# A hand-ordered attention trunk on one core: other places for single instructions, output stores by halves

## The chip, the cores and the metric

The kernel runs on one core of one Trainium2 chip. The metric is the device time of one execution in microseconds (us): 1213.29 us before the change, the median of three runs (1212.85 to 1214.43). TensorE (PE in the profile) multiplies matrices, with its weight loads shown apart (PEld). VectorE is DVE, ScalarE is ACT, GpSimd is POOL, and SyncE (SP) issues most DMAs. Each engine works through its own list of instructions in order; semaphores join the lists.

## The reference, cut to what matters

Two layers over 16 meta tokens and 1024 tokens, width 1024. Each layer adds to h the product of w_out with two gated attention groups; at the end comes one more norm.

```
def hybrid_layer(h, pos, norm_g, w_in, w_out, sinks):
    u = rmsnorm(h, norm_g)
    proj = jnp.einsum('bld,de->ble', u, w_in)
    sb_q, sb_k, sb_v, sb_g, sw_q, sw_k, sw_v, sw_g = jnp.split(proj, splits, axis=-1)
    sb_o = stick_breaking_attention(sb_q, sb_k, sb_v) * silu(sb_g)      # 8 heads, strictly causal
    qr, kr = rope(sw_q, pos), rope(sw_k, pos)
    sw_o = sliding_window_gqa(qr, kr, sw_v, sinks) * silu(sw_g)         # window 128, sinks
    mix = jnp.concatenate([sb_o, sw_o], axis=-1)
    return h + jnp.einsum('ble,ed->bld', mix, w_out)

def reference(...):
    h = concatenate([meta, x])
    for l in range(2):
        h = hybrid_layer(h, pos, norm_g[l], w_in[l], w_out[l], sinks[l])
    return rmsnorm(h, final_norm_g)[:, 16:]
```

## The kernel before, in words

Tokens lie along the free dimension, in three chunks of 400, 384 and 256 (c = 0, 1, 2); features lie on partitions. Weights come in tiles of 128 output features: 26 for w_in, then 8 for w_out. Every projection of a tile on a chunk is done to nearly full float32 precision by three passes over 8 row blocks k: high weights times high input, high weights times low input, low weights times high input, so 24 matmuls. The input's halves are UH and UL, the weights' are WH and WL. A tile's weights are split on VectorE by split_w (line 1424): a CAST to WH (line 1430), then WL as the rest (line 1434). This pair is called the weight pair below. The norm scales a chunk in four parts of two row blocks: "scale" on VectorE (line 1382), "high" on ScalarE (the copy to UH, line 1092), "low" on VectorE (UL, line 1392). The first projection of a layer asks for the four UL parts one after another, each before two of its row blocks.

One list of steps per layer (layer_steps, line 137) sets the order of everything. Each engine walks the same list and issues its own share of each step, so moving a step in the list moves its instructions on every engine that has a part in it. The list follows these stages:

1. First projections (v, g of pair 0), with the norm of the chunks between them. In layer 0 the input is also transposed (in_turn), copied (in_copy: half on ScalarE, half on VectorE), squared for the norm (in_square, ScalarE) and the norm's numbers spread over partitions (in_row, on TensorE). start_steps orders layer 0's start.
2. Stick-breaking attention over 4 pairs of heads, with the next projections merged in.
3. Sliding stage (swa_attention, line 209): 18 units, 9 for each head pair. A unit n has the scores SZ on TensorE; on VectorE the peak (3 or 5 small instructions, lines 1562 to 1570); on ScalarE the exponentials (line 1269); on VectorE the weighing SD (4 instructions, lines 1578 to 1587); on TensorE the turn ST and the values SAV; on VectorE the taking of the result. Between them stand projections (one for each unit, two for the first), rotations (rope_add, rope_high, rope_low) and the weight pairs of later tiles. Near its end stand gates and the splitting of the attention's result into UH and UL, which are the input of w_out.
4. Output projections, each with "add" (h is updated, line 1453; the semaphore h_ready counts 24 of them in a layer), squares and their sum. At the layer boundary boundary_steps puts the next layer's norm of chunk 0 between the last projections.
5. Tail (out_steps): final norm, a transposing matmul for each block of 128 tokens (out_turn, line 1043), scaled copies of the two halves of its 1024 columns (ScalarE the first 512, VectorE the last 512), and one store of 512 KB a block.

WITHIN names small matmuls that stand inside a projection, by row block. proj_slot (line 825) makes the second layer's first two projections wait for the last add of the layer before.

## Time and profile before

| | |
|---|---|
| median of three runs | 1213.29 us (1212.85 to 1214.43) |
| the profiled execution's own time | 1215.04 us |
| its span, first to last instruction | 1213.2 us |
| PE busy | 1174.4 us, 97% |
| DVE busy | 688.3 us, 57% |
| ACT busy | 435.8 us, 36% |

The span leaves out 1.8 us that lie around the instructions. With TensorE busy 97% of the span, its idle time is small: about 39 us in some forty places, and the places matter more than the sums. A row of the timeline shows the idle time just before an instruction in brackets, with the instruction or DMA that ended it.

### The profile page before, as it was taken

The numbers are of one execution on the slowest core, as the hardware profiler recorded it, in microseconds if no ns is written. First come the engines' busy times: TensorE is split into PE (matmuls) and PEld (weight loads), VectorE is DVE, ScalarE is ACT, GpSimd is POOL, SyncE is SP. The second block draws the span as 40 slices with busy tenths as digits, with TensorE's granted clock in tenths as the row PEclk, the third lists the DMA queues.
The fourth block names the chain that finished last, engine by engine and source line by source line (L and its number), as shares of the span: only waits on it lengthen the run. The fifth ranks groups of instructions, "written<-read, shape, count | busy, mean of one in ns | idle before, by whom it ended". The sixth has DMA issues, their size and how long they took to land.

```text
span 1213.2 us, 22513 instructions
## 1 busy us (share of the span) xinstructions
PE 1174.4 (97%) x8922; PEld 1074.2 (89%) x8922; DVE 688.3 (57%) x1370; ACT 435.8 (36%) x1189; POOL 2.6 (0%) x5
## 2 busy tenths in 40 slices
PE   6999999999999999999989999999999999999998
PEld 6988888988888888899989888888888888888998
DVE  6646464455457567754574564655544855766533
ACT  7323333333344344521231333333334433554113
POOL 0000000000000000000000000000000000000000
PEclk9999999999999999999999999999999999999999
DMA  6611010101021021141321110101011212104203
GB/s 213 219 36 36 19 36 18 36 19 36 21 56 44 23 57 50 41 172 35 141 70 54 34 36 19 36 19 36 18 36 25 64 36 45 49 14 171 70 5 140
DMA packets 101687, 69.31 MB, mean 57 GB/s; under 512 B 37824, under 2 KB 95168, under 8 KB 101584
## 3 DMA queue, kind: packets, MB, share of 16 engines
q1 hardware_dynamic: 100720, 66.55, 18.2%
q8 instruction: 72, 1.18, 0.4%
q10 hardware_dynamic: 864, 1.32, 0.4%
q14 instruction: 31, 0.25, 0.1%
HBM read 49.82 MB, written 12.71 MB: 52 GB/s over the span
## 4 chain that ended last, share of the span: by engine, by line
PE 89%; DVE 5%; issue 2%; ACT 2%; DMA 1%; SPq 0%; ACTq 0%; DVEq 0%
PE psum L867 41%; PE psum L855 20%; PE psum L917 7%; PE psum L946 6%; PE psum L929 6%; PE psum L978 2%; PE psum L1043 1%; PE psum L990 1%; PE psum L1015 1%; PE psum L1008 1%; DVE mix L1382 1%; DMA vT<-in_x 1%; PE psum L959 1%; PE psum L888 1%; DVE UL L1392 1%
## 5 line engine op out<-in xcount | busy, mean ns | idle before, releaser
L867 PE MATMUL psum<-UH,WH 128*128 128x384 f32 (+2 forms) x1632 | 538.5, 330 | 10.1 <-DVE UL L1392 4.9
L867 PE MATMUL psum<-UL,WH 128*128 128x384 f32 (+2 forms) x1632 | 524.6, 321 | 0.0
L855 PE MATMUL psum<-UH,WL 128*128 128x384 f32 (+2 forms) x1632 | 517.9, 320 | 0.0
L867 PEld LDWEIGHTS psum<-UH,WH 128*128 128x128 f32 x1632 | 308.4, 189 | 19.9 <-issue 9.0
L867 PEld LDWEIGHTS psum<-UL,WH 128*128 128x128 f32 x1632 | 309.1, 189 | 0.1
L855 PEld LDWEIGHTS psum<-UH,WL 128*128 128x128 f32 x1632 | 308.3, 189 | 0.0
L1255 ACT ACTIVATE PT<-psum 128x512 f32<-128x512 f32 (+5 forms) x260 | 116.7, 492 | 20.0 <-PE psum L929 18.3
L1246 ACT ACTIVATE X<-psum 128x264 f32<-128x264 f32 (+9 forms) x240 | 91.1, 431 | 78.2 <-PE psum L917 77.8
L1514 DVE TENSOR_TENSOR_SCAN X<-X,stick 16x16 f32<-16x16 f32 (+5 forms) x144 | 100.4, 736 | 24.7 <-ACT X L1246 24.3
L929 PE MATMUL psum<-ident,X 128*128 128x128 f32 x576 | 91.1, 283 | 3.7 <-ACT Vn L1209 2.7
L1517 DVE TENSOR_TENSOR_SCAN X<-X 128x352 f32<-128x352 f32 (+4 forms) x96 | 86.3, 939 | 7.7 <-ACT X L1246 7.7
L929 PEld LDWEIGHTS psum<-ident,X 128*128 128x128 f32 x576 | 61.9, 141 | 27.4 <-issue 23.1
L946 PE MATMUL psum<-PT,Vn 128*64 128x128 f32 (+1 forms) x1152 | 83.8, 281 | 0.0
L1434 DVE TENSOR_TENSOR WL<-w_raw,WH 128x1024 fp32r<-128x1024 f32 x67 | 82.1, 1226 | 2.3
L946 PEld LDWEIGHTS psum<-PT,Vn 128*64 128x64 f32 (+1 forms) x1152 | 61.1, 136 | 18.4 <-issue 18.2
L1137 ACT ACTIVATE mix<-X 128x400 f32<-128x400 f32 (+2 forms) x48 | 23.3, 493 | 130.0 <-DVE X L1453 127.8
L1453 DVE TENSOR_TENSOR X<-psum,X 128x400 f32<-128x400 f32 (+2 forms) x48 | 24.8, 517 | 77.0 <-PE psum L855 76.8
L1544 DVE SCALAR_TENSOR_TENSOR mix<-psum,v_end,mix 128x128 f32<-128x128 f32 (+1 forms) x72 | 23.9, 332 | 78.1 <-PE psum L959 78.0
L1430 DVE CAST WH<-w_raw 128x1024 fp32r<-128x1024 f32 x68 | 46.6, 685 | 24.3 <-issue 14.5
L917 PE MATMUL psum<-qk_even 64*128 64x264 f32 (+9 forms) x360 | 46.3, 342 | 3.7 <-DVE qk_even L1467 2.0
L917 PE MATMUL psum<-qk_odd 64*128 64x264 f32 (+9 forms) x360 | 46.4, 342 | 2.2 <-ACT X L1246 1.7
L1467 DVE TENSOR_TENSOR qk_even<-psum,qk_even 128x400 fp32r<-128x400 f32 (+2 forms) x24 | 12.4, 519 | 60.5 <-ACT qk_even L1164 32.0
(171 smaller groups left out, 1000.7 us busy)
## 6 DMA issues: line engine op xcount, KB each, us to landing
w_raw<-in_w_in SPq DMA_DIRECT2D x36, 512.0 KB, 3.8
h_spill<-X SPq DMA_DIRECT2D x16, 520.0 KB, 6.5
X<-h_spill SPq DMA_DIRECT2D x16, 520.0 KB, 5.2
w_raw<-in_w_in SPq DMA_DIRECT2D x32, 256.0 KB, 3.7
w_raw<-in_w_out SPq DMA_DIRECT2D x16, 256.0 KB, 2.9
w_raw<-in_w_out SPq DMA_DIRECT2D x32, 128.0 KB, 3.2
vT<-dvT SPq DMA_DIRECT2D x40, 50.0 KB, 2.0
vT<-dvT SPq DMA_DIRECT2D x40, 48.0 KB, 2.0
```

What stands on the lines that cost most here:

```text
L855: return pe.matmul(out_columns, WL[:, j % 2, k, :], UH[:, k, uses], start=False, stop=(k == KT - 1))
L867: pe.matmul(out_columns, WH[:, j % 2, k, :], u[:, k, uses], start=(k == 0 and u is UH), stop=False)
L917: ins = pe.matmul(z_bank[0:n_queries(b), h, 0:hi - lo], QK[rows, q, queries], QK[rows, k, lo:hi], start=(i == 0), stop=(i == 2))
L929: ins = pe.transpose(bank[:, i * nq:(i + 1) * nq], weights(p, b, h)[:, a:a + 128], ident[:])
L946: ins = pe.matmul(o[64 * h:64 * h + 64, 0:nq], Vn[keys, 9 * (p % 2) + t, 64 * h:64 * h + 64], PT[keys, slots[h] % PT_RING, i * nq:(i + 1) ...
L1246: act.activation(weights(p, b, h)[0:n_queries(b), lo:hi], z_bank[0:n_queries(b), h, 0:hi - lo], ACT.Sigmoid, scale=-SCALE).then_inc(z_read ...
L1255: act.activation(PT[0:rows, slot % PT_RING, 0:width], t_bank[use % T_RING][0:rows, 0:width], ACT.Copy)\
L1430: dve.tensor_copy(WH[:, j % 2, :, :], w_raw[:, j % 2, :, :]).then_inc(wh_made.sem, 1)
L1434: dve.tensor_tensor(WL[:, j % 2, :, :], w_raw[:, j % 2, :, :], WH[:, j % 2, :, :].bitcast(F32), ALU.subtract).then_inc(wl_made.sem, 1)
L1453: dve.tensor_tensor(X[:, t, chunk_uses(c)], proj_bank[use % 2][:, 0:CHUNKS[c][1]], X[:, t, chunk_uses(c)], ALU.add).then_inc(h_ready.sem, 1)
L1514: ins = dve.tensor_tensor_scan(down, down, edge, 1.0, ALU.mult, ALU.max)
L1517: ins = dve.tensor_tensor_scan(down, down, down, P[0:nq, hi:hi + 1], ALU.mult, ALU.bypass)
```

## The change

Five kinds of edits, with no arithmetic changed.

- Start of layer 0: ScalarE's squares stand behind the "high" copies they stood ahead of; the row of norm numbers of chunk 1 goes into the last pass of the first projection; the second tile's weight pair is pulled apart, with its second half behind two parts of the next norm.
- Layer boundary: the norm numbers of chunk 1 and the CAST of tile 0 move ahead of the last two UL parts, with WL behind them; the second tile's WL moves behind chunk 1's scaling; the first projection of layer 1 waits for the 23rd add and not for the 24th.
- Opening of the sliding stage: the scores of units 0 and 1 each stand ahead of the projection they stood behind.
- Sliding stage: the weight pairs of tiles up to the first of w_out move from behind a unit's values to behind the next unit's weighing. There are five such pairs in each layer.
- Tail: the last sums stand between the halves of block 7's turn; each store is split in two of 256 KB, the first waiting for ScalarE's half alone.

```diff
@@ start_steps
-    spread = {c0[0]: [S[4]], c0[2]: [S[5]], c0[4]: [C[4]], c0[5]: [S[6]], c0[7]: [C[5]], c0[8]: [S[7]], c0[10]: [S[8]]}
+    spread = {c0[2]: [S[4]], c0[4]: [C[4]], c0[5]: [S[5]], c0[7]: [C[5]], c0[8]: [S[6]], c0[10]: [S[7], S[8]]}
...
-    steps += [C[6], ("in_root", 1), ("in_refine", 1)] + v[0] + [T[8], ("in_row", 1), ("in_row", 2), ("split_w", 1)]
-    spread = {c1[1]: [C[7]], c1[6]: g[0], c1[8]: [C[8]]}
+    steps += [C[6], ("in_root", 1), ("in_refine", 1), ("split_w", 1, "high")] + v[0] + [T[8], ("in_row", 2)]
+    spread = {c1[1]: [("split_w", 1, "low"), C[7]], c1[6]: g[0], c1[8]: [C[8]]}
@@ layer_steps
-            start = [("split_w", 1)] + v[0] + c1[:4] + [("norm", 2, 0)] + c1[4:7] + g[0] + c1[7:]
+            start = [("split_w", 1, "high")] + v[0] + c1[:3] + [("split_w", 1, "low")] + c1[3:4] + [("norm", 2, 0)]
+            start += c1[4:7] + g[0] + c1[7:]
@@ swa_attention
-        out = fill[0] + [("SZ", 0), ("SD", 0)] + fill[1] + [("SZ", 1)]
-        fill = fill[2:]
+        out = [("SZ", 0), ("SD", 0)] + fill[0] + [("SZ", 1)] + fill[1]
+        fill, weights_next = fill[2:], []
...
-            out += extra.get(n, []) + ropes + [step for step in task if step not in late + ropes]
+            out += extra.get(n, []) + ropes + weights_next + [step for step in task if step not in late + ropes]
...
-            out += [("SAV", n)] + late
+            weights_next = [step for step in late if step[0] == "split_w" and step[1] <= IN_TILES]
+            out += [("SAV", n)] + [step for step in late if step not in weights_next]
...
-    tail[0] = flush + tail[0]
-    steps += swa_attention(tail + [[("proj", IN_TILES + i, c)] for i, c in EARLY_OUTS])
+    steps += flush + swa_attention(tail + [[("proj", IN_TILES + i, c)] for i, c in EARLY_OUTS])
@@ boundary_steps
-            (KT - 1, 1): c0[5:],
-            (KT - 2, 2): [("norm", 1, 1), ("split_w", TILES)]}.get((i, c), [])
+            (KT - 1, 1): c0[5:8] + [("norm", 1, 1), c0[8]],
+            (KT - 2, 2): [("split_w", TILES, "high")] + c0[9:] + [("split_w", TILES, "low")]}.get((i, c), [])
@@ out_steps
-            (KT - 1, 2): [("out_turn", 7), ("out_sum", 2), ("out_root", 2), ("out_copy", 7)] + blocks(8, 9)}.get((i, c), [])
+            (KT - 1, 2): [("out_turn", 7), ("out_root", 2), ("out_copy", 7)] + blocks(8, 9)}.get((i, c), [])
@@ WITHIN
-          ("proj", 0, 0): {4: [("norm_row", 1, 0), ("in_turn", 6)], 6: [("in_turn", 7)]},
+          ("proj", 0, 0): {4: [("norm_row", 1, 0), ("in_turn", 6)], 6: [("in_turn", 7)], KT + 5: [("in_row", 1)]},
@@ sync, the stores
                 sp.wait_ge(out_ready_a, b)
+                sp.dma_start(out[128 * (b - 1):128 * b, 0:512], staged_out(b)[:, 0:512]).then_inc(out_stored, 16)
                 sp.wait_ge(out_ready_v, b)
-                sp.dma_start(out[128 * (b - 1):128 * b, :], staged_out(b)).then_inc(out_stored, 16)
-            sp.wait_ge(out_stored, 16 * (BLOCKS - 1))
+                sp.dma_start(out[128 * (b - 1):128 * b, 512:1024], staged_out(b)[:, 512:1024]).then_inc(out_stored, 16)
+            sp.wait_ge(out_stored, 32 * (BLOCKS - 1))
@@ proj_slot
-                        pe.wait_ge(h_ready.sem, h_ready.at(l, 0))
+                        pe.wait_ge(h_ready.sem, h_ready.at(l, use - 1))
@@ project, in the last pass
+                            if l == 0 and KT + k in WITHIN.get(step, {}):
+                                in_rows(1)
@@ out_turn
+                        if b == 7 and half == 0:
+                            out_sums(2)
@@ split_w: part "high" is the CAST with its waits, part "low" the rest
-                def split_w(j):
+                def split_w(j, part=None):
```

The order of VectorE at the layer boundary, before. X<-psum is an add, small<-psum and small<-small refine the norm numbers of chunk 1, dvT<-dvT,mix sums squares.

```order
L1382 SCALAR_TENSOR_TENSOR mix<-X,par,psum 128x400
L1392 TENSOR_TENSOR UL<-mix,UH 128x2x400 [waits u_scaled,uh_made] x2
L1453 TENSOR_TENSOR X<-psum,X 128x256 [waits h_back0,proj_full]
L1363 SCALAR_TENSOR_TENSOR small<-psum,small 128x3 [waits rooted]
L1366 SCALAR_TENSOR_TENSOR small<-small 128x3 [waits refined]
L1369 SCALAR_TENSOR_TENSOR small<-small 128x3 [waits refined]
L1430 CAST WH<-w_raw 128x1024 [waits wl_made,proj_full,w_landed0]
L1434 TENSOR_TENSOR WL<-w_raw,WH 128x1024 [waits wl_made,wh_made]
L1453 TENSOR_TENSOR X<-psum,X 128x256 [waits h_back1,proj_full]
```

And the same place in the changed kernel.

```order
L1388 SCALAR_TENSOR_TENSOR mix<-X,par,psum 128x400
L1369 SCALAR_TENSOR_TENSOR small<-psum,small 128x3 [waits rooted]
L1372 SCALAR_TENSOR_TENSOR small<-small 128x3 [waits refined]
L1375 SCALAR_TENSOR_TENSOR small<-small 128x3 [waits refined]
L1460 TENSOR_TENSOR X<-psum,X 128x256 [waits h_back0,proj_full]
L1437 CAST WH<-w_raw 128x1024 [waits wl_made,proj_full,w_landed0]
L1398 TENSOR_TENSOR UL<-mix,UH 128x2x400 [waits u_scaled,uh_made] x2
L1441 TENSOR_TENSOR WL<-w_raw,WH 128x1024 [waits wl_made,wh_made]
L1460 TENSOR_TENSOR X<-psum,X 128x256 [waits h_back1,proj_full]
```

The numbers, the 23rd add and the CAST now stand ahead of the last two UL parts; the 24th add still comes last.

VectorE near the end of the sliding stage of layer 0, before: the taking of unit 13's values, the weight pair of w_out's first tile, the weighing of unit 15, the last UL part of chunk 0, the gate and the peak of unit 16.

```order
L1604 COPY mix<-psum 128x2x128 [waits av_done]
L1430 CAST WH<-w_raw 128x1024 [waits wl_made,proj_full,w_landed0]
L1434 TENSOR_TENSOR WL<-w_raw,WH 128x1024 [waits wl_made,wh_made]
L1578 TENSOR_TENSOR small<-small 128x4 [waits z_read,sink_exp]
L1579 RECIPROCAL small<-small 128x4 [waits dve_order]
L1583 TENSOR_TENSOR P_late<-P_late,small 128x4x16 [waits dve_order]
L1587 TENSOR_TENSOR P_late<-P_late,small 128x4x128 [waits dve_order]
L1618 TENSOR_TENSOR UL<-mix,UH 128x2x400 [waits mh_made]
L1479 SCALAR_TENSOR_TENSOR X<-X,psum 128x256 [waits g_act]
```

And the same place in the changed kernel.

```order
L1611 COPY mix<-psum 128x2x128 [waits av_done]
L1585 TENSOR_TENSOR small<-small 128x4 [waits z_read,sink_exp]
L1586 RECIPROCAL small<-small 128x4 [waits dve_order]
L1590 TENSOR_TENSOR P_late<-P_late,small 128x4x16 [waits dve_order]
L1594 TENSOR_TENSOR P_late<-P_late,small 128x4x128 [waits dve_order]
L1625 TENSOR_TENSOR UL<-mix,UH 128x2x400 [waits mh_made]
L1437 CAST WH<-w_raw 128x1024 [waits wl_made,proj_full,w_landed0]
L1441 TENSOR_TENSOR WL<-w_raw,WH 128x1024 [waits wl_made,wh_made]
L1486 SCALAR_TENSOR_TENSOR X<-X,psum 128x256 [waits g_act]
```

The weight pair has moved behind the weighing and the UL part, and stands between them and the gate.

## Rows read from the trace of the kernel before

**Rows 1.** The page: busy us of each engine (share of the span) xinstructions.

```profile
PE 1174.4 (97%) x8922; PEld 1074.2 (89%) x8922; DVE 688.3 (57%) x1370; ACT 435.8 (36%) x1189; POOL 2.6 (0%) x5
```

**Rows 2.** TensorE's waits, whole span: who, for whom, us in total, times, longest.

```profile
PE psum L867 <- issue: 3.2, 1, 3.2
...
PE psum L990 <- DVE P_early L1587: 2.2, 2, 1.1
...
PE psum L867 <- DVE X L1453: 2.0, 2, 1.0
PE psum L978 <- DVE SQ L1552: 1.9, 2, 1.0
PE psum L978 <- ACT P_late L1269: 1.3, 2, 0.7
...
PE psum L978 <- ACT P_early L1269: 0.7, 2, 0.5
```

**Rows 3.** Windows: PE, PEld, DVE, ACT, POOL busy us (instructions), granted clock, DMA, GB/s.

```profile
613.30:616.70 3.40, 3.40 (x13) 3.27 (x12) 2.86 (x5) 0.00 (x0) 0.00 (x0) 0.50 1.02 308
463.10:466.50 3.40, 3.40 (x19) 3.35 (x17) 2.81 (x9) 2.38 (x11) 0.00 (x0) 0.50 0.11 29
```

**Rows 4.** Timeline, layer boundary: start, us, instruction, xcount, [idle before, releaser].

```profile
606.78 2.02 DVE L1392 TENSOR_TENSOR UL<-mix,UH 128x800 fp32r<-128x800 f32 x2
609.77 0.16 DVE L1363 SCALAR_TENSOR_TENSOR small<-psum,small 128x3 f32<-128x3 f32 x1 [0.64 <-ACT small L1084]
612.14 0.42 DVE L1453 TENSOR_TENSOR X<-psum,X 128x256 f32<-128x256 f32 x1
612.66 0.42 PE L867 MATMUL psum<-UH,WH 128*128 128x400 f32 x1 [3.18 <-issue]
615.83 2.19 DVE L1382 SCALAR_TENSOR_TENSOR mix<-X,par,psum 128x384 f32<-128x384 f32 x4 [0.50 <-PE psum L794]
623.96 0.34 PE L867 MATMUL psum<-UH,WH 128*128 128x384 f32 x1
```

**Rows 5.** The weight pair's two instructions, whole span: ns min/median/max, first and last start.

```profile
L1430 DVE CAST WH<-w_raw x68: 655/684/695, 11.7 to 1170.4; 128x1024 fp32r<-128x1024 f32 x68
L1434 DVE TENSOR_TENSOR WL<-w_raw,WH x67: 1224/1226/1227, 24.3 to 1171.1; 128x1024 fp32r<-128x1024 f32 x67
```

**Rows 6.** Timeline, opening of the sliding stage, layer 0.

```profile
395.30 0.64 DVE L1552 TENSOR_TENSOR SQ<-dvT,SQ 128x16 fp32r<-128x16 f32 x2
395.69 0.45 PE L867 MATMUL psum<-UH,WH 128*128 128x400 f32 x1
407.36 0.66 PE L990 MATMUL psum<-ident,P_early 128*128 128x128 f32 x4 [1.11 <-DVE P_early L1587]
```

**Rows 7.** Timeline, end of the sliding stage, layer 0.

```profile
503.85 0.68 DVE L1430 CAST WH<-w_raw 128x1024 fp32r<-128x1024 f32 x1
505.22 0.85 ACT L1255 ACTIVATE PT<-psum 128x512 f32<-128x512 f32 x2
505.71 0.15 DVE L1578 TENSOR_TENSOR small<-small 128x4 f32<-128x4 f32 x1
506.98 0.98 DVE L1618 TENSOR_TENSOR UL<-mix,UH 128x800 fp32r<-128x800 f32 x1
508.11 0.42 PE L867 MATMUL psum<-UH,WH 128*128 128x400 f32 x1
522.77 0.44 PE L867 MATMUL psum<-UH,WH 128*128 128x384 f32 x1 [0.97 <-DVE X L1453]
```

**Rows 8.** Timeline, start of layer 0.

```profile
15.06 0.99 DVE L1392 TENSOR_TENSOR UL<-mix,UH 128x800 fp32r<-128x800 f32 x1 [0.55 <-ACT UH L1092]
18.69 0.45 PE L867 MATMUL psum<-UH,WH 128*128 128x400 f32 x1 [1.52 <-DVE UL L1392]
```

**Rows 9.** DMA issues: out<-in, queue, xcount, KB each, median us to landing.

```profile
out<-w_raw SPq DMA_DIRECT2D x1, 512.0 KB, 3.0
vT<-dvT SPq DMA_DIRECT2D x40, 50.0 KB, 2.0
```

More of the change, by code:

```diff
@@ L757, in _ @@
                 for step in LAYER_STEPS[l]:
-                    if step[0] == "split_w" and step[1] + 2 < TILES:
+                    if step[0] == "split_w" and step[1] + 2 < TILES and step[2:] != ("high",):
                         load(step[1] + 2)
@@ L1422, in _ @@
                 link = chain.link
-                def split_w(j):
-                    dve.wait_ge(w_landed[j % 2].sem, w_landed[j % 2].at(l + j // TILES, landed(j % TILES)))
-                    if j >= 2:
-                        dve.wait_ge(proj_full.sem, proj_full.at(l, PROJ_AT["proj", j - 2, 2] + 1))
-                    if l or j >= 2:
-                        dve.wait_ge(wl_made.sem, wl_made.at(l, j - 1))
-                    dve.tensor_copy(WH[:, j % 2, :, :], w_raw[:, j % 2, :, :]).then_inc(wh_made.sem, 1)
-                    if l or j:
+                def split_w(j, part=None):
+                    if part != "low":
+                        dve.wait_ge(w_landed[j % 2].sem, w_landed[j % 2].at(l + j // TILES, landed(j % TILES)))
+                        if j >= 2:
+                            dve.wait_ge(proj_full.sem, proj_full.at(l, PROJ_AT["proj", j - 2, 2] + 1))
+                        if l or j >= 2:
+                            dve.wait_ge(wl_made.sem, wl_made.at(l, j - 1))
+                        dve.tensor_copy(WH[:, j % 2, :, :], w_raw[:, j % 2, :, :]).then_inc(wh_made.sem, 1)
+                    if (l or j) and part != "high":
                         dve.wait_ge(wh_made.sem, wh_made.at(l, j + 1))
@@ L1657, in _ @@
                     elif kind == "split_w":
-                        split_w(step[1])
+                        split_w(*step[1:])
                     elif kind == "norm":
```

## The prediction, written before the changed kernel had run

> **What bounds the kernel now.** Read the page first: TensorE is busy 97% of the span, 1174.4 us of 1213.2 [rows 1]. Nothing in the change takes a matmul away, so all it can give is part of TensorE's idle time, some 39 us, and whatever time a low clock adds. So the second view is the list of TensorE's waits [rows 2]. The edits touch these: 3.2 us at the layer boundary; 2.2 and 0.7 at the opening of the sliding stage; 1.9 in its middle; 1.3 and 2.0 at its end. Except for the first, each is two waits, one in each layer. The third view is the windows [rows 3]: twice, for 3.4 us each, the granted clock is 0.50, that is 1.2 GHz for 2.4. Such a stretch does half its work, so it costs 1.7 us. One stands right behind the 3.2 us wait at the boundary, the other behind the wait in the middle of layer 0's sliding stage. Last comes the timeline of VectorE at each place, since VectorE ends most of these waits: there the question is whether VectorE itself waits (then its order can be mended) or is busy all through (then moving work only moves the bill).
>
> **Layer boundary: -3.6 us.** TensorE ended layer 0's last projection at 612.66 - 3.18 = 609.5 and began layer 1's first at 612.66, right behind the add that VectorE began at 612.14 [rows 4]. The profile names no releaser, but the code has the wait: the 24th h_ready. That add came late because two UL parts (2.0 us from 606.8), the chunk's numbers (which waited 0.64 for ScalarE), a weight pair and another add stood ahead of it. Now TensorE wants only the 23rd add and the CAST. VectorE from 606.8: three small instructions to 607.4, the 23rd add (0.42) to 607.8, CAST (0.69) to 608.5 [rows 4, 5]. Both are there at 609.5, so this wait ends at nothing. The two UL parts end at 609.5 and 610.4; they are wanted by the fifth and seventh of eight row blocks, 1.5 us and 2.5 us into the projection: in time. WL ends at 611.6, wanted after 16 matmuls at about 612.7: in time. The 24th add ends near 612.0, wanted at 614: in time.
>
> What is late next: on VectorE follow the sums (0.8, to 612.8), CAST (613.4), four scalings (2.19, to 615.6), the WL that was moved behind them (616.8), a UL part (0.96, to 617.8) and chunk 2's numbers (0.6, to 618.4). The second projection wants those numbers before its last row block. Before, the two projections took 623.96 - 612.66 = 11.3 us, 1.7 of it the low clock's: 9.6 at full clock. From 609.5 TensorE would be through at 619.1, and at that row block about 2.1 us sooner, at 617.0. So it waits 1.4 us and is through at 620.4, against 623.96: 3.6 us gained, the 1.7 of the clock included. Bounds: 4.9 (3.2 + 1.7, the new wait hidden) and 1.9 (the new wait brings a low stretch of its own).
>
> **Opening of the sliding stage: -2.4 us.** With unit 0's scores ahead of a projection, the chain scores, peak, exponentials, weighing (11.7 us from 395.69 to the turn at 407.36, with two projections in it) runs beside one projection more. Its two waits in each layer, 2.9 us in both [rows 2], go. The price: the scores need the low half of a rotated query, which VectorE ends at 395.30 + 0.64 = 395.94, and TensorE is there at 395.69 [rows 6]; 0.25 a layer. The tanh and the gates of the moved projections stand behind the exponentials, but the projection that wants their bank begins five microseconds later. Value 2.4; bounds 0 (the chain is only moved) and 2.9.
>
> **Middle: -1.9 us, and the clock's 1.7 in this execution.** The wait is for a rotation's low half (L1552). A weight pair, 0.68 + 1.23 = 1.91 us [rows 5], stood ahead of it on VectorE and now stands behind it. The wait was 0.96, so it goes whole in both layers: 1.9 [rows 2]. The pair ends 1.9 us later, ahead of a wait for scores that VectorE had there anyway. In layer 0 the low stretch from 463.1 goes with the wait [rows 3]; I count it apart, since layer 1's equal wait had none. Bounds 0 and 1.9.
>
> The Trainium skill (TensorE: Matmul & The Clock Gate, "What's actually happening") says that the gate's window runs free of the program. By that, equal waits may or may not meet a low stretch, and this trace's two agree. It changes no term; it speaks for the spread of a run's time.
>
> **End of the sliding stage: +3.2 us.** Here the same move costs. Before, VectorE did the pair of w_out's first tile from 503.85, while ScalarE was still at the exponentials (it went on to the next work at 505.22); the weighing began at 505.71, just behind the pair [rows 7]. Now VectorE idles until the exponentials are done, about 505.4, weighs (1.35) and does the UL part (0.98, to 507.7), and only then the pair: CAST to 508.4, WL to 509.6. TensorE wants that very tile at 508.11, so it waits 0.3 for WH and 0.8 for WL. And VectorE has from there no slack: gate, peak, second pair, weighing, two UL parts, peak follow each other without a break, and end in the add for which TensorE waits 0.97 at 522.77 [rows 7]. All of it comes 1.91 - 0.3 = 1.6 us later, and TensorE's 1.1 us of waits lie inside that. So 1.6 a layer, 3.2. Bounds: 0 and 3.8 (both pairs whole). The other four moved pairs of a layer stand where projections leave VectorE room: 0, or with that room gone 1.6 each.
>
> **Start of layer 0: -0.5 us.** VectorE waited 0.55 for ScalarE's UH, which stood behind a square [rows 8]; that square is now behind. VectorE then ends each UL part about 0.55 sooner, and TensorE's wait of 1.52 for one shrinks as much. The row of numbers in the last pass finds them only just ready (0.3 lost, made good by VectorE's earlier scaling). Bounds 0 and 0.8.
>
> **Tail: -0.7 us.** The earlier sums free block 7's copies, but the last copy waits for the same last matmul. What is left is the last store: 256 KB for 512, with the first half already gone. 512 KB landed in 3.0 us and 50 KB in 2.0 [rows 9]; on the line between, 256 KB take 2.4. Without the store of block 7 beside it, some 0.1 less. Bounds 0 and 1.0.
>
> The Trainium skill (DMA: Bandwidth & Descriptors, "Bandwidth") tells you to batch DMAs into larger ones. By that rule halving would be a loss; with these rows only the last landing counts, and 2.0 of its 3.0 us are there at 50 KB too.
>
> **The sum.** 3.6 + 2.4 + 1.9 - 3.2 + 0.5 + 0.7 = 5.9 us. The profiled execution took 1215.04: 1213.2 of span and 1.8 around it. It held the low stretch in the middle as well, 1.7: 1215.04 - 5.9 - 1.7 = 1207.4. The median, 1213.29, is 1.75 below the profiled time, about one low stretch; if it lacks that one, 1213.29 - 5.9 = 1207.4 too.
>
> **Rivals.**
> First, the clock: the change leaves new waits of about 1.4 us at the boundary and 1.1 us (beside an old 0.65) in each layer's end. For it: two of the waits named above had a low stretch behind them. Against: layer 1's middle wait and the openings' had none. Two or three such stretches more, at 1.7: 1207.4 + 4.3 = 1211.7.
> Second, the boundary gives half: some other wait holds the first projection (a UL part, a weight), or the new wait is longer. For it: VectorE is busy all through. Against: every wanted thing had over a microsecond of room, except the numbers. Gain 1.9 for 3.6: 1209.1.
> Third, the end costs nothing, since TensorE or ScalarE sets the pace there: 1204.2. Against: the rows show VectorE without a break.
> Fourth, the other side: VectorE has no room at any moved pair. Five pairs in two layers at 1.6 are 16 us; with all else as above (5.9 + 3.2 + 1.7 = 10.8 gained) 1215.04 - 10.8 + 16 = 1220.2. It decides once seven or more of the ten are exposed, which makes the total slower. Against: the profile names a wait of TensorE for VectorE at no other unit [rows 2], and the projections between them are long.
>
> **How the numbers follow.** Forecast 0.52 (1205.5 to 1209.0), clock 0.18, boundary half 0.13, end free 0.11, pairs exposed 0.06. From the few runs at hand 0.2%, 2.4 us, is about what can be told from no change: faster is below 1210.9, slower above 1215.7. Faster holds the forecast, the second and the third rival, and half of the first: 0.86; same 0.09; slower 0.05. The range from 1204.0 to 1211.5 leaves out the fourth rival, the upper part of the first, and little below.
>
> **What would show it.** Right: no 3.2 us wait at the boundary, but one of 1 to 1.5 us inside the second projection, ahead of the numbers' transposes; no waits for P_early and SQ; at w_out's first tile new waits on WH and WL, and the wait for the add about 1.5 us; stores of 256 KB, the last landing in 2.2 to 2.4. Wrong: VectorE's add at the boundary not earlier than 612, a weighing in units 2 to 9 for which TensorE waits, or the end of the sliding stage as long as before.

## The result, and the profile after

The changed kernel takes 1205.2 us (median of four runs, 1204.28 to 1208.14), the kernel before beside it 1213.86; the ratio is 0.9933, with a 95% interval of 0.9913 to 0.9953. Five later runs gave 1205.46 and 0.9937 [0.9925, 0.9949]. The interval lies below 1 as a whole, so the kernel is faster, by 0.7%. The forecast was 1207.4, range 1204.0 to 1211.5. The profiled execution took 1204.28 us, its span 1202.5, that is 10.7 less than before.

The page's first line: TensorE has 4.9 us less of busy time than in [rows 1], with the same number of instructions. That is no work saved; a matmul in a low-clock stretch is busy for longer.

```profile
PE 1169.5 (97%) x8922; PEld 1069.6 (89%) x8922; DVE 688.1 (57%) x1370; ACT 435.7 (36%) x1189; POOL 2.6 (0%) x5
```

TensorE's waits in the changed kernel (who, for whom, us in total, times, longest), to set beside [rows 2]:

```profile
PE psum L869 <- DVE UL L1398: 4.5, 4, 1.7
...
PE psum L869 <- DVE X L1460: 2.9, 2, 1.4
...
PE psum L857 <- DVE WL L1441: 1.3, 2, 0.6
...
PE psum L796 <- DVE small L1375: 0.6, 1, 0.6
...
PE psum L982 <- DVE SQ L1559: 0.5, 2, 0.2
PE psum L869 <- DVE WH L1437: 0.2, 1, 0.2
```

The 3.2 with no releaser is gone, and so are both for P_early; SQ fell from 1.9 to 0.5, and that 0.5 now stands at the opening. New are the waits for the numbers (small), WL and WH; the one for the add (X) grew from 2.0.

Such a list adds up named waits. To size each part I cut both traces at the same TensorE rows. First rows of the kernel before that were not shown yet: the third UL part of chunk 1 in the start, the last 0.51 wait of the stick-breaking stage of layer 0, the sliding stage's wait for P_late, the sums ahead of the boundary, the same UL part behind it, then layer 1, and the first turn of the tail.

```profile
35.19 0.45 PE L867 MATMUL psum<-UH,WH 128*128 128x384 f32 x1 [1.67 <-DVE UL L1392]
...
347.04 0.63 PE L929 MATMUL psum<-ident,X 128*128 128x128 f32 x4 [0.51 <-ACT Vn L1224]
...
505.49 0.33 PE L978 MATMUL psum<-SKH,SQ 64*128 64x144 f32 x2 [0.65 <-ACT P_late L1269]
...
604.64 0.62 PE L784 MATMUL psum<-ones,dvT 128*128 128x16 f32 x4 [0.48 <-DVE dvT L1445]
...
627.24 0.44 PE L867 MATMUL psum<-UH,WH 128*128 128x384 f32 x1 [1.02 <-DVE UL L1392]
...
936.63 0.63 PE L929 MATMUL psum<-ident,X 128*128 128x128 f32 x4 [0.51 <-ACT Vn L1224]
...
1091.82 0.33 PE L978 MATMUL psum<-SKH,SQ 64*128 64x144 f32 x2 [0.65 <-ACT P_late L1269]
...
1108.83 0.45 PE L867 MATMUL psum<-UH,WH 128*128 128x384 f32 x1 [1.02 <-DVE X L1453]
...
1204.66 0.60 PE L1043 MATMUL psum<-Vn,X 128*128 128x128 f32 x3 [0.51 <-DVE X L1453]
```

And the same places in the changed kernel; 518.16 is the add that stood at 522.77 in [rows 7].

```profile
34.62 0.44 PE L869 MATMUL psum<-UH,WH 128*128 128x384 f32 x1 [1.67 <-DVE UL L1398]
...
344.89 0.63 PE L933 MATMUL psum<-ident,X 128*128 128x128 f32 x4 [0.51 <-ACT Vn L1230]
...
499.25 0.34 PE L982 MATMUL psum<-SKH,SQ 64*128 64x144 f32 x2 [0.66 <-ACT P_late L1275]
...
518.16 0.44 PE L869 MATMUL psum<-UH,WH 128*128 128x384 f32 x1 [1.41 <-DVE X L1460]
...
599.98 0.84 PE L786 MATMUL psum<-ones,dvT 128*128 128x16 f32 x6 [0.48 <-DVE dvT L1452]
...
618.31 0.44 PE L869 MATMUL psum<-UH,WH 128*128 128x384 f32 x1 [1.03 <-DVE UL L1398]
...
927.67 0.52 PE L933 MATMUL psum<-ident,X 128*128 128x128 f32 x3 [0.51 <-ACT Vn L1230]
...
1080.29 0.33 PE L982 MATMUL psum<-SKH,SQ 64*128 64x144 f32 x2 [0.65 <-ACT P_late L1275]
...
1098.92 0.44 PE L869 MATMUL psum<-UH,WH 128*128 128x384 f32 x1 [1.44 <-DVE X L1460]
...
1194.79 0.94 PE L1047 MATMUL psum<-Vn,X 128*128 128x128 f32 x6 [0.52 <-DVE X L1460]
```

Low-clock stretches of 3.4 us, in windows (busy times of the engines, then the granted clock): the kernel before had two besides those of [rows 3], one at 12.5 us and this one.

```profile
73.95:77.35 3.40, 3.40 (x12) 3.36 (x11) 1.63 (x9) 0.00 (x0) 0.00 (x0) 0.50 0.52 154
```

The changed kernel had one, in the start (this window is a little off its edges, so the clock reads 0.54); the boundary ran at 1.00.

```profile
12.50:15.90 3.40, 2.62 (x13) 2.63 (x14) 3.40 (x6) 2.32 (x5) 2.37 (x1) 0.54 1.02 406
604.60:608.00 3.40, 3.40 (x22) 3.35 (x21) 3.25 (x6) 0.42 (x1) 0.00 (x0) 1.00 0.25 99
```

The differences of the rows, with 1.7 us (half of 3.4) taken out for each stretch that one trace has and the other not:

| place | before | after | waits | forecast |
|---|---|---|---|---|
| start, to the UL part | 35.19 | 34.62 | -0.57 | -0.5 |
| opening and middle, layer 0 | 158.45 (1.7 of it clock) | 154.36 | -2.39 | -2.15 |
| opening and middle, layer 1 | 155.19 | 152.62 | -2.57 | -2.15 |
| end, layer 0 | 17.28 | 18.91 | +1.63 | +1.6 |
| end, layer 1 | 17.01 | 18.63 | +1.62 | +1.6 |
| boundary | 22.60 (1.7 of it clock) | 18.33 | -2.57 | -1.9 |
| tail, to the span's end | 8.54 | 7.71 | -0.83 | -0.7 |
| sum of waits | | | -5.7 | -4.2 |
| stretches at 74, 463, 613 us | | | -5.1 | -3.4 |

Everything between these places is the same to 0.05 us, but for the place with the stretch at 74 us: from the UL part to the stick-breaking stage's last wait it took 311.85 us and now takes 310.27, so this stretch cost 1.58 and not 1.7. Other pairs of profiles of which one has a stretch give 1.5 to 1.6 as well. At 1.58 each the clock's share of the 10.7 us is 4.7 and that of the waits 6.0: a little more than half is waits, the rest is clock. The table keeps the 1.7.

The mean clock of a run tells how many stretches it had: one takes 0.0014 off it (3.4 x 0.5 of 1205 us). The nine runs of the changed kernel have 0.9977 on average, 1.6 stretches; sixteen runs of the kernel before, taken beside the later five, have 0.9958, 3.0 stretches. So over many runs the clock gives about 1.4 stretches, 2.2 us, and not the three of this pair of profiles. With the 6.0 us of waits that makes 8.2; the medians are 7.9 apart (1213.32 and 1205.46).

### The profile page after: what moved, and what is told of

Read it like the earlier page. It is cut to its first block, busy times and chain, and to the rows that moved or that the text cites. A ratio compares the mean times of both kernels' runs of the same rounds, so it can differ in the third digit from the quotient of the medians.

```text
span 1202.5 us, 22513 instructions
## 1 busy us (share of the span) xinstructions
PE 1169.5 (97%) x8922; PEld 1069.6 (89%) x8922; DVE 688.1 (57%) x1370; ACT 435.7 (36%) x1189; POOL 2.6 (0%) x5
## 4 chain that ended last, share of the span: by engine, by line
PE 89%; DVE 6%; ACT 2%; issue 2%; DMA 0%; SPq 0%; ACTq 0%; DVEq 0%
PE psum L869 41%; PE psum L857 20%; PE psum L921 7%; PE psum L933 6%; PE psum L950 6%; PE psum L982 2%; PE psum L1047 1%; DVE mix L1388 1%; PE psum L1019 1%; PE psum L994 1%; PE psum L1012 1%; DVE UL L1398 1%; PE psum L963 1%; ACT P_late L1275 1%; PE psum L892 1%
## 5 line engine op out<-in xcount | busy, mean ns | idle before, releaser
L1474 DVE TENSOR_TENSOR qk_even<-psum,qk_even 128x400 fp32r<-128x400 f32 (+2 forms) x24 | 12.5, 519 | 60.5 <-ACT qk_even L1170 31.9
```

## The experiments

Two numbers are read of each: the median with its ratio to the kernel before, and the same places in its profile. From kernel to kernel the end, the boundary and the tail repeat within 0.03 us, where they are unchanged; opening and middle within 0.6; the start within 0.5 (34.41 to 34.85 us in seven profiles with the changed start and an early stretch), since the input doesn't land at the same time in each (TensorE's first wait for it ends between 3.39 and 3.92 us there). The runs of one kernel differ by several us, so the profile is the sharper tool. The runs were made in four series, each with its own runs of the kernel before, whose medians differ by up to 1.7 us: medians are compared inside a series, ratios across them.

| kernel | median us | before beside it | ratio [95%] |
|---|---|---|---|
| after_again | 1205.46 | 1213.32 | 0.9937 [0.9925, 0.9949] |
| end_undone | 1200.87 | 1213.32 | 0.9911 [0.9895, 0.9926] |
| boundary_undone | 1208.93 | 1213.32 | 0.9968 [0.9955, 0.9980] |
| opening_undone | 1208.73 | 1213.32 | 0.9967 [0.9956, 0.9978] |
| before_pairs | 1213.68 | 1213.75 | 0.9997 [0.9987, 1.0008] |
| start_undone | 1206.80 | 1213.75 | 0.9942 [0.9928, 0.9956] |
| tail_whole | 1205.11 | 1213.75 | 0.9931 [0.9920, 0.9943] |
| boundary_wait24 | 1207.31 | 1215.04 | 0.9932 [0.9918, 0.9946] |
| boundary_filled | 1209.40 | 1215.04 | 0.9954 [0.9940, 0.9968] |
| boundary_filled13 | 1209.81 | 1214.34 | 0.9960 [0.9946, 0.9973] |
| best_order | 1199.87 | 1213.75 | 0.9891 [0.9875, 0.9907] |
| best_warm | 1201.85 | 1214.34 | 0.9893 [0.9880, 0.9907] |

**The changed kernel again.**

> The changed kernel as it is, for more runs beside those of the parts. The theory (waits removed, about 5.6 us, and fewer low-clock stretches at 1.7 us each) expects a ratio to the kernel before of 0.993 to 0.995, near 1205.5 us, with runs that differ among themselves by steps of about 1.7 us as the mean clock falls from 0.999. The rival (the gain is mostly clock, and luck) expects runs spread over both kernels' times, with a ratio nearer 0.997.

Runs at 1204.3, 1204.6, 1205.5, 1205.9 and 1206.1, ratio as the theory had it. The lower two have a mean clock of 0.998, the others 0.997, so the time does follow the clock, but not in clean steps of 1.7.

**The end of the sliding stage.**

```diff
-            weights_next = [step for step in late if step[0] == "split_w" and step[1] <= IN_TILES]
+            weights_next = [step for step in late if step[0] == "split_w" and step[1] < IN_TILES]
```

> The changed kernel, but the weight pair of w_out's first tile stays behind the values of its unit, where the kernel before had it; the other four pairs of a layer are moved as in the change. The theory (VectorE has no slack there, so the pair's move costs 1.2 to 1.6 us in each layer) expects 2.4 to 3.2 us less than the changed kernel, about 1202.5 us: the waits of TensorE for WL (0.63 and 0.64) and WH (0.2) at w_out's first tile go, and the wait for the add falls from 1.41 and 1.44 back to about 0.97. The rival (TensorE or ScalarE sets the pace at the end of the sliding stage) expects no difference, 0.5 us either way: the same waits come back under another name.

TensorE's two rows of layer 0 in this kernel's timeline:

```profile
501.31 0.34 PE L982 MATMUL psum<-SKH,SQ 64*128 64x144 f32 x2 [0.67 <-ACT P_late L1275]
...
518.61 0.45 PE L869 MATMUL psum<-UH,WH 128*128 128x384 f32 x1 [0.99 <-DVE X L1460]
```

17.30 us between them, as before the change (17.28), for 18.91 with it; layer 1 gives 17.02. The pair's move costs 1.6 us a layer, 3.2 in all. The median is 4.6 lower; the rest of that is clock, since three of the five runs have a mean clock of 0.999 or 1.000, for 0.997 and 0.998 in after_again. The rival that the end costs nothing is out. In the changed kernel VectorE's rows at this place are:

```profile
499.21 0.16 DVE L1585 TENSOR_TENSOR small<-small 128x4 f32<-128x4 f32 x1 [1.51 <-ACT P_late L1275]
...
501.39 0.69 DVE L1437 CAST WH<-w_raw 128x1024 fp32r<-128x1024 f32 x1
502.11 1.23 DVE L1441 TENSOR_TENSOR WL<-w_raw,WH 128x1024 fp32r<-128x1024 f32 x1
...
512.85 0.16 DVE L1585 TENSOR_TENSOR small<-small 128x4 f32<-128x4 f32 x1 [1.51 <-ACT P_late L1275]
```

VectorE idles 1.51 us at 499.21 where it had done the pair, and does the pair when TensorE wants it. (The second wait, at 512.85, was there before the change as well; more on it below.) The list of waits shows only 2.4 of the 3.2 us (WL 1.3, WH 0.2, the add 0.9 more); the cut between equal rows shows all.

**The boundary, undone whole and by its one wait.** The first goes back to the three pieces of code that the change's diff shows for the boundary; the second is one line:

```diff
-                        pe.wait_ge(h_ready.sem, h_ready.at(l, use - 1))
+                        pe.wait_ge(h_ready.sem, h_ready.at(l, 0))
```

> The changed kernel with the layer boundary of the kernel before: norm numbers of chunk 1 and the CAST behind the UL parts, the second tile's pair in one piece, and layer 1's first projection waiting for the 24th add. The theory expects 2.6 to 3.2 us more of waits (the 3.2 us wait is back, the wait of 0.6 for chunk 2's numbers goes) and, when a low-clock stretch stands behind the wait as it did in the profile before, 1.7 more: 1208.2 to 1210.0 us. The rival that the boundary gives half expects 1.9 at most; a second rival, that the low stretch at the boundary was chance, expects its 1.7 us in fewer than half of the runs.

> The changed kernel with one thing undone at the boundary: layer 1's first projection waits for the 24th add again, with VectorE's new order kept. In the changed kernel's trace that add ends at 606.88 and TensorE is there at 604.6, so the theory expects a wait of 2.2 us, the wait of 0.6 for the numbers of chunk 2 gone, and 1.6 us more in all: 1207.0 us. That would make the wait for the 23rd add worth 1.6 of the boundary's 2.6, and VectorE's order the other 1.0. The rival that the order alone carries the gain (the 24th add is early enough) expects nothing. On the clock: if a low-clock stretch follows waits of TensorE of over 2 us, one stands near 608 us of this profile and the time is 1.7 more.

With the boundary undone, timeline and window:

```profile
600.20 0.84 PE L785 MATMUL psum<-ones,dvT 128*128 128x16 f32 x6 [0.48 <-DVE dvT L1451]
608.21 0.43 PE L868 MATMUL psum<-UH,WH 128*128 128x400 f32 x1 [3.21 <-issue]
622.81 0.44 PE L868 MATMUL psum<-UH,WH 128*128 128x384 f32 x1 [1.03 <-DVE UL L1397]
```

```profile
608.50:611.90 3.40, 3.40 (x13) 3.26 (x12) 2.54 (x4) 0.07 (x1) 0.00 (x0) 0.51 0.89 266
```

With the one wait alone:

```profile
599.52 0.84 PE L786 MATMUL psum<-ones,dvT 128*128 128x16 f32 x6 [0.48 <-DVE dvT L1452]
606.52 0.44 PE L869 MATMUL psum<-UH,WH 128*128 128x400 f32 x1 [2.19 <-issue]
621.11 0.44 PE L869 MATMUL psum<-UH,WH 128*128 128x384 f32 x1 [1.02 <-DVE UL L1398]
```

22.61 and 21.59 us from the sums to the UL part, for 18.33, each with a low stretch behind the wait. Without its 1.7 that is 2.6 for the whole and 1.56 for the one wait, 1.6 forecast: with the new order in place the line in proj_slot brings 1.6, and VectorE's order alone brings the other 1.0. The new line on the old order was not run. boundary_undone's median is 3.5 above the changed kernel's. That of boundary_wait24 shows nothing: its ratio, 0.9932, is the changed kernel's 0.9937 within both intervals, so its 1.6 rests on the profile alone.

**The opening.** Both lines of the change's diff on the opening taken back:

> The changed kernel with the opening of the sliding stage as before: unit 0's scores behind the first projection, unit 1's behind the second. The theory expects TensorE's waits for P_early back, 2.2 for the weighing and 0.7 for the exponentials over both layers, less the 0.5 us that the new order waits for SQ: 2.4 us more than the changed kernel, 1207.6 us. The rival (the chain is only moved, and what TensorE waits there is caught up at the next unit) expects 0.5 us at most.

```profile
PE psum L995 <- DVE P_early L1595: 2.3, 2, 1.1
```

Both waits are back, that for the exponentials too, and the medians differ by 3.3 us. In layer 1, from the stick-breaking stage's last wait to that for P_late:

```profile
930.27 0.63 PE L934 MATMUL psum<-ident,X 128*128 128x128 f32 x4 [0.51 <-ACT Vn L1231]
...
1084.70 0.34 PE L983 MATMUL psum<-SKH,SQ 64*128 64x144 f32 x2 [0.65 <-ACT P_late L1276]
```

154.43 us for 152.62: 1.8 in this layer, while 1.2 was forecast. In layer 0 the same place takes 155.33 us (344.93 to 500.26) for 154.36: 1.0. That is 2.8 in both layers for 2.4 forecast. The place varies from profile to profile by 0.5 to 0.6 in each layer (152.61 to 153.08 in layer 1), so the 0.4 between them says nothing.

**The pairs alone, on the kernel before.**

```diff
-            out += [("SAV", n)] + late
+            weights_next = [step for step in late if step[0] == "split_w" and step[1] <= IN_TILES]
+            out += [("SAV", n)] + [step for step in late if step not in weights_next]
```

(and weights_next behind the ropes, as in the change)

> The kernel before with one part of the change alone: the five weight pairs of a layer, up to the first of w_out, move behind the next unit's weighing. The theory expects the middle's two waits for SQ to go (-1.9 us) and the end to cost 1.2 us in each layer (+2.3, the waits for WL, WH and a longer wait for the add): +0.4 us against the kernel before, less 1.7 in those runs in which the middle's low-clock stretch goes too, so 1212 to 1214 us. The rival that VectorE has no room at any moved pair expects 5 to 13 us more. The rival that the middle's waits are only moved expects +2.3. The 3.2 us wait at the boundary is still there; if such waits bring the low stretch that stands behind them, one is seen near 613 us of this profile too.

```profile
933.83 0.41 PE L930 MATMUL psum<-ident,X 128*128 128x128 f32 x2 [0.51 <-ACT Vn L1225]
...
1087.99 0.34 PE L979 MATMUL psum<-SKH,SQ 64*128 64x144 f32 x2 [0.65 <-ACT P_late L1270]
...
1106.60 0.44 PE L868 MATMUL psum<-UH,WH 128*128 128x384 f32 x1 [1.43 <-DVE X L1454]
```

154.16 us for 155.19 before: the middle gives 1.03 in this layer, and the end costs 1.60 (18.61 for 17.01). Layer 0 agrees: 155.72 us (345.43 to 501.15) for 158.45 less the clock's 1.7 is 1.03 too. The other pairs cost nothing: that rival, with its 5 to 13 us, is out. By the waits the part alone loses 1.2 us; its median is the same as before's (0.9997); its eleven runs have a mean clock of 0.9966 on average for 0.9954 in the kernel before beside it, almost one stretch less, which makes up for the waits. So one edit holds a gain of 2.1 us and a loss of 3.2.

**Start and tail.** The start's lines of the diff taken back, and the stores whole again:

> The changed kernel with layer 0's start as before: squares ahead of the high copies, the row of numbers of chunk 1 behind the first projection, the second tile's pair in one piece ahead of chunk 1's scaling. The theory expects TensorE's wait for the third UL part back at 1.5 us from 1.0 and everything behind it 0.5 us later: 0.5 us more in the profile's span at equal clock. The rival expects nothing, since DMAs of the input set the pace of the start. The medians of five runs can't tell the two apart; the place of the first chunk-1 matmul behind the wait for UL (34.62 us in the changed kernel, 35.19 before) can.

> The changed kernel with whole output stores of 512 KB, each behind both halves' copies. The theory expects the last landing at 2.9 to 3.0 us instead of 2.4, nothing else: 0.5 to 0.6 us more between the last copy and the end of the span. The rival (bytes in flight of the blocks before it set the end, so the halves only share the same bandwidth) expects no difference; another, that twice as many issues on the queue cost time, expects the whole stores to be faster by 0.3.

The start's profile had a stretch at 19 us and another at 36, so its UL part at 35.97 can't be set beside 34.62. It can be set beside the two with the changed start that have a stretch at 19 as well: end_undone's 35.39, a difference of 0.58, and boundary_filled13's 35.18, a difference of 0.79. Between before and after it was 0.57. So the start gives some 0.6, from places that vary by up to 0.4 themselves. In tail_whole, the first turn and the last store:

```profile
1194.91 0.82 PE L1046 MATMUL psum<-Vn,X 128*128 128x128 f32 x5 [0.52 <-DVE X L1459]
```

```profile
out<-w_raw SPq DMA_DIRECT2D x1, 512.0 KB, 2.6
```

From the turn to the span's end at 1203.1 are 8.19 us, for 7.71 with halves (256 KB in 2.4) and 8.54 before. So the halves bring 0.48 and the rest of the tail 0.35. The whole last store landed in 2.6 us here and in 3.0 in [rows 9], and up to the last copy both kernels take 5.1 us from the turn, so the 0.35 is all in the landing. Block 7's store is issued 1.8 us ahead of the last one here, 0.9 us before the change; that it was this store which slowed the last one fits, but no run shows it by itself. The ratios (0.9931 and 0.9937) show nothing of 0.5 us.

**Does the wait bring the low clock?** In four profiles TensorE waited 2.2 or 3.2 us at the boundary, and all four had a stretch right behind; in the profiles without that wait there was none there. So I filled the wait, in the kernel with the boundary undone, with matmuls whose result is overwritten: first 26, then 13.

```diff
+                    if l and (j, c) == (0, 0):
+                        pe.wait_ge(h_ready.sem, h_ready.at(l, -1))
+                        for _ in range(13):
+                            pe.matmul(proj_bank[0][:, 0:128], ident[:, 0:128], ident[:, 0:128], start=True, stop=True)
```

> The kernel with the boundary undone (3.2 us wait at its 24th add, low-clock stretch right behind it), and 26 extra matmuls of the identity with itself, 128x128, on TensorE inside that wait; their results are overwritten. At 0.12 us each, as the final turns' matmuls take, they fill some 3 us from 605.0 us on. The theory that the wait's idleness brings the low stretch at this place expects the stretch near 608 us to be gone, and about 1.7 us less than the kernel with the boundary undone: a profile of 1208.5 for 1210.3, a median near 1207.5 for 1208.9. The rival (the stretch at this place is chance, or follows the long busy time before it) expects the stretch still there in the profile and the same median. A third outcome, that the extra matmuls outlast the wait, shows as a first projection that begins after 608.3.

> The same fill of the boundary's wait with half as many extra matmuls, 13: the 26 took 5.97 us and outlasted the wait by 2.4 us. At 0.23 us each they now end at about the same time as the wait for the 24th add (3.2 us). The theory that an idle TensorE brings the low-clock stretch at this place expects no stretch near 608 us and 1.7 us less than the kernel with the boundary undone: the lowest runs near 1207.0, the median 1207.2 for 1208.93. The rival expects the stretch in the profile and the same median, 1208.9.

The 26 ran from 604.70 until the first projection at 610.42 and outlasted the wait (sums to UL part 23.42 us, no stretch). With 13, timeline and window:

```profile
602.15 0.84 PE L785 MATMUL psum<-ones,dvT 128*128 128x16 f32 x6 [0.48 <-DVE dvT L1455]
606.82 3.06 PE L846 MATMUL psum<-ident 128*128 128x128 f32 x26
...
623.18 0.44 PE L872 MATMUL psum<-UH,WH 128*128 128x384 f32 x1 [1.02 <-DVE UL L1401]
```

```profile
610.20:613.60 3.40, 3.40 (x20) 3.35 (x21) 3.21 (x6) 0.32 (x1) 0.00 (x0) 1.00 0.80 236
```

The stretch is gone from the boundary, and the place takes 21.03 us for 22.61: 1.6 less, for 1.7 expected. But the time did not fall (ratio 0.9960, and 0.9968 unfilled, with intervals that overlap): there were other stretches, at 19 and 74 us in the profile, and the mean clock of all runs, 0.996 to 0.997, is that of the unfilled kernel. Here the expectation missed. With 26, all five runs had 0.999 to 1.000, one stretch at most.

So in profiles the stretch at the boundary was there four times of four with the wait empty, and not at all in the two with it filled. The empty wait doesn't bring it every time, though: one run of before_pairs, which has the 3.2 us wait, took 1210.94 us at a mean clock of 1.000, and one of boundary_wait24, with the 2.2 us wait, 1205.88 us at 1.000, which leaves no room for a stretch anywhere. Idleness there makes the stretch likely; what decides in the single execution, and how many fall elsewhere, stays open.

**A better order.** The pair of w_out's first tile left where it was, and:

```diff
-            start = [("split_w", 1, "high")] + v[0] + c1[:3] + [("split_w", 1, "low")] + c1[3:4] + [("norm", 2, 0)]
-            start += c1[4:7] + g[0] + c1[7:]
+            start = [("split_w", 1, "high")] + v[0] + c1[:3] + [("split_w", 1, "low"), ("norm", 2, 0)] + c1[3:4]
+            start += c1[4:10] + g[0] + c1[10:]
...
-    spread = {c1[1]: [("split_w", 1, "low"), C[7]], c1[6]: g[0], c1[8]: [C[8]]}
+    spread = {c1[1]: [("split_w", 1, "low"), C[7]], c1[9]: g[0], c1[11]: [C[8]]}
```

> The changed kernel with four further moves: the pair of w_out's first tile back where the kernel before had it (-2.4 us, as its own run showed in the waits); at the boundary the norm numbers of chunk 2 ahead of the first UL part of chunk 1 (the wait of 0.6 goes); there and in layer 0's start the taking of the gate projection behind the third UL part, and in the start also the copy of block 8 behind the fourth. The theory (VectorE's order sets the waits of TensorE for UL, 1.0 at the boundary and 1.7 in the start) expects the boundary's two waits to shrink by 1.4 together and the start's by 1.3: in all 5.1 us less than the changed kernel, about 1200.4 us. The rival (TensorE is stopped a little later by another UL part or by the bank that the late taking frees) expects only the 2.4 of the pair: 1203.

```profile
600.48 0.84 PE L786 MATMUL psum<-ones,dvT 128*128 128x16 f32 x6 [0.48 <-DVE dvT L1452]
617.35 0.45 PE L869 MATMUL psum<-UH,WH 128*128 128x384 f32 x1 [0.36 <-DVE UL L1398]
618.99 0.44 PE L869 MATMUL psum<-UH,WH 128*128 128x384 f32 x1 [0.32 <-DVE UL L1398]
```

1199.87 us, 5.2 below the 1205.11 of tail_whole in the same series, and 1.1% below the kernel before; the changed kernel is 0.6 to 0.7% below it. The pair brings its 3.2; the third UL part comes 1.46 sooner after the sums (16.87 us for 18.33), but the fourth is now late by 0.32, so the boundary gives 0.9 and not 1.4, and the start 0.4 (by the first wait behind it, at 71.99 and 72.43 us in end_undone, both with a stretch near 18). That is 4.5 us of waits. 5.1 were expected, from other parts: 2.4 for the pair, 1.4 for the boundary, 1.3 for the start.

**Filling the start's waits.**

> The kernel of best_order, and 17 extra matmuls of the identity with itself, without use for the result, inside five waits of layer 0's start: 5 ahead of block 1's turn (wait 1.46 us), 3 ahead of the first row of numbers (0.94), 4 ahead of block 4's turn (1.26), 3 and 2 ahead of the first projection's second and third UL part (1.03 and 0.72). At 0.23 us each they fit. Every profile so far has one low-clock stretch between 12 and 20 us. The theory that these waits bring it expects it to be gone or shorter, and up to 1.7 us less than best_order's lowest runs: 1197.8 to 1198.5; less than 1.7 since TensorE waits there for VectorE and the input anyway. The rival, that the first long wait for the input (3.4 us) brings it or that it falls by a rhythm of its own, expects the stretch still there and 1199.5 to 1199.9, or 0.3 more where a transfer of the input comes early and finds TensorE in the extra work.

The stretch between 12 and 20 us is gone in the profile (one stood at 74), and the UL part comes at 34.09 for 34.35; yet the ratio, 0.9893, is best_order's 0.9891. A miss. The fastest run, 1200.45 us, has a mean clock of 1.000, and best_order's at 0.999 take 1199.4 to 1199.9: with no stretch at all the filled kernel is no faster. In this pair of profiles losing the stretch was worth 0.3 us and not 1.7, which fits that TensorE waits there for the input and for VectorE anyway; but the extra matmuls may cost something themselves, and the input came 0.7 us later in best_order's profile, so the 0.3 is no clean price.

## Why the prediction held, step by step

- **Boundary** (3.6 forecast, the clock's 1.7 in it; 4.3 measured). The mechanism was right: the first projection follows the last with no gap, and the new wait stands inside the second projection. Mis-sized was that wait, 0.61 us for 1.4:

```profile
604.62 0.35 PE L869 MATMUL psum<-UH,WH 128*128 128x400 f32 x1
...
613.01 0.43 PE L796 MATMUL psum<-ident,small 128*128 128x128 f32 x2 [0.61 <-DVE small L1375]
```

The numbers were ready 8.4 us after the first projection began, for 8.9 forecast. I had laid VectorE's durations end to end, but in the timeline consecutive instructions overlap by up to 0.1 (the 24th add starts at 606.46 and takes 0.42, the next one starts at 606.79), and some twenty stand in this chain. That is 0.5 of the 0.8 us; the other 0.3 is that TensorE itself came to that row block later than forecast. The second rival (half the gain) is out.
- **Opening** (2.4 forecast; 2.9 measured: 4.96 for opening and middle over both layers, less the middle's 2.06; undone alone 2.8). The price, 0.25 a layer for SQ, was right, though the list of signs then said "no waits" for it. The 0.5 above the forecast is no more than this place varies from profile to profile.
- **Middle** (1.9; 2.06 measured on its own).
- **End** (+3.2; +3.25 measured, and undone alone 3.2). One reason given was misread: VectorE is not busy without a break up to the add. It waits at the last weighing, before the change as after it (512.85 above):

```profile
517.47 0.16 DVE L1578 TENSOR_TENSOR small<-small 128x4 f32<-128x4 f32 x1 [1.52 <-ACT P_late L1269]
```

That the cost came out whole all the same shows that this wait is no slack. It is for exponentials which follow VectorE's own peak, so a later peak moves it along: it is 1.52 and 1.51 us long.
- **Start and tail** (0.5 and 0.7; 0.57 and 0.83). In the tail the block 7 store weighed 0.35 for the 0.1 I gave it.
- **Clock.** The forecast took two stretches off the profile and got three. The third, at 74 us, was luck: the wait ahead of it is 1.02 us in both kernels. That the one in the middle went with its wait is not shown either; layer 1's equal wait had none. A stretch was also priced too high, 1.7 for 1.5 to 1.6 measured. At full clock the profiles say 1215.04 - 4 x 1.7 = 1208.2 before and 1204.28 - 1.7 = 1202.6 after. The medians lie 5 and 2.6 to 2.9 us above, about three and one and a half stretches: an estimate, since a stretch in the start costs less, but the mean clocks of the runs say the same. The first rival had the sign of the total wrong: there are fewer stretches, not more. Its mechanism is seen all the same, now and then. Of the twenty waits of about 1.4 us for the add (ten profiles with the moved pair, two layers), two had a stretch of their own: it began 0.1 us behind the one at 1103.40 us in boundary_undone and 0.1 us before the end of the one at 520.95 in start_undone. The eight waits of 1.0 us for the same add had none. The Trainium skill (TensorE: Matmul & The Clock Gate, "What's actually happening") says that the gate's window runs free of the program. The runs agree in part: the same waits met a stretch in one execution and not in the next (the two runs at a mean clock of 1.000 above), and yet at the boundary the stretch was there in every profile with the wait unfilled.

Two sums of the prediction are off without touching the forecast. The chances for "faster" add up to 0.85 and not 0.86. And seven exposed pairs would give 1204.24 + 7 x 1.6 = 1215.4 us, just short of the 1215.7 from which "slower" was counted; it takes eight.

So 1207.4 was 2.2 us too high: 1.5 of it waits (boundary 0.7, opening and middle 0.7), the rest clock. The waits that go and come were named rightly; the mis-sized term is the boundary's new wait, 0.61 us for 1.4.

## What to carry to other kernels

Ask of every moved instruction what its engine did at the old place: the same move of a weight pair gave 1 us where it stood in front of something wanted, and cost 1.6 where it had filled the engine's wait for another one. When a wait of the busiest engine goes, sum the follow-up work up to the next thing that it wants; that sum found the new wait to 0.8 us. And where runs differ by more than the effects, compare profiles between equal rows, with clock stretches counted apart; the list of waits showed 2.4 of the 3.2 us that one edit cost.

## What the runs showed of the hardware

- The granted clock fell to 0.50 (1.2 GHz for 2.4) for stretches of 3.4 us, one to four in a profile. Waits of 2.19 us (one profile) and 3.2 us (three) were followed by one. Where TensorE is busy one costs 1.5 to 1.6 us (311.85 us for 310.27, 22.61 for 21.03), in the start less (0.3 in one pair of profiles).
- A stretch at 74 us stood behind a wait of 1.02 us in five profiles of fourteen; the equal wait in layer 1, near 656 us, had one in four. The same wait has it in one execution and not in the next.
- 13 calls of a float32 matmul of 128x128 stand in the timeline as 26 instructions and took 3.06 us, 0.235 a call and 0.12 an instruction. The final turns' rows count instructions too, 24 in 2.92 us, 0.12 each. I had priced the filler at 0.12 a call and was out by two.
